# Gate products of a recurrent block as four 64x64 tiles, and a new order of transposes and conversions around them

## The chip, the cores and the metric

The kernel runs on one core of a Trainium2 chip. Its metric is the device time of one execution in microseconds; three executions of the kernel before give 296.25 us (median; 296.24 to 296.85). TensorE, VectorE, ScalarE, GpSimd and the DMA queue of SyncE each run their own list of instructions in order and meet at semaphores.

## The reference

One transformer layer on 256 tokens of width 1024, all in float32. Cut to what matters here:

```python
h = rms_norm(x, mix_norm_g)
xr, yg, q, k, v = split(h @ w_in)                      # 5 parts of 512 channels
xr = causal_depthwise_conv(xr, lru_conv_w, lru_conv_b)
r = sigmoid(einsum('bshi,hij->bshj', xh, w_a) + b_a)   # 8 heads, a 64x64 matrix each
i = sigmoid(einsum('bshi,hij->bshj', xh, w_i) + b_i)
a = exp(-8 * r * softplus(-lam));  u = sqrt(1 - a*a) * (i * xr)
y_lru = scan(a, u) * gelu(yg)                          # h[t] = a[t] h[t-1] + u[t]
y_attn = causal attention of 8 heads of 64 with distance slopes, q and k normed
x = x + concat(rms_norm(y_lru), rms_norm(y_attn)) @ w_out
x = x + (gelu(gate) * value) @ w_down                  # from rms_norm(x) @ w_up, convolved
```

## The kernel before, in words

Every weight matrix comes in units of 128 x 1024 numbers (0 to 93), two to a DMA of SyncE. A unit u is split into two parts of lower precision: `hi(u)` on ScalarE (L355) and `lo(u)` on VectorE (L652 and L656); VectorE makes both parts of units 17 to 22. A product of float32 accuracy is then three fast matmuls (`three`, L1001, L1002, L1005). TensorE waits for `lo_done` before it uses a unit. Units 0 to 7 are q and k, 8 to 11 the recurrent input, 12 to 15 the GELU branch y, 16 to 19 v, 20 to 27 w_out, 28 on the feed-forward part, whose loop takes the time behind 112 us.

The order of each engine is written out by hand. Around the change it is as follows.

TensorE computes y unit 0, then the gate products (`gates_product`, L1102): for each chunk c of 128 channels (two heads) one float32 matmul for the gate r and one for the gate i, with a 128x128 stationary operand that holds the two heads' 64x64 matrices on its diagonal and zeros elsewhere, and 256 tokens as columns. Both go to one PSUM bank, `X_ACC[c]`, r in columns 0 to 255, where the recurrent input of the chunk was until the convolution (`conv_rest`, L731) had read it. Then come pairs of heads' scores (`score_pair`, two heads on the two halves of the rows), y units, v units and the transposes of the probabilities (`transpose_p(h)`, L1099, three 128x128 blocks of a head). `score_pair(h)` waits until `shift` of the heads before has read the banks.

A head's probabilities pass these steps: `shift(h)` on VectorE (L746: add the distances, row minimum), `exps(h)` on ScalarE (L430), the division by the row sum (on GpSimd, L345, for heads 0 to 3; `row_scale(h)` on VectorE, L758 and L761, for the others), `transpose_p(h)` on TensorE, and `p_out(h)` on ScalarE (L436), the copy out of PSUM. The probabilities have five slots, so `shift(5)` waits for the transpose of head 0 (semaphore `pT`), `shift(6)` for that of head 1 and `shift(7)` for that of head 2. The transposed heads share two banks: `transpose_p(h)` waits for `p_out(h - 2)`.

The recurrence passes these: sigmoids on ScalarE (L471 and L473); `gate_i * xc` on VectorE (L801, `lru_in`); decay and tanh on ScalarE (L479, L480), their square (L485, `a2_done`); on VectorE the product that gives 1 - a^2 up to the sign (L807); the root on ScalarE (L494); on VectorE (L818, L820, L824) the scan's input, four scans and the product with GELU (`y_done`). `y_to_hi(c)` (L503) and `y_to_lo(c)` (L829) split chunk c of it for w_out and count `mix_ready`; `y_sq` (L515) and `chunk_sums` (L834, L835) give the sums of squares, which `y_sums` on TensorE adds up at w_out's second unit. For the attention half the same is done by L524, `chunk_sums` again (`a_chunks`) and `a_sums` (L1166) at the third unit. `v_out(m)` (L511) copies v out of PSUM; the second half of the attention products (`attend`, L1188) waits for `v_out(1)`.

Behind w_out, `f_add` (L879) adds the result to x, its norm follows, and `transpose_f` (L1222) turns it for the feed-forward part.

Of the kernel before, what the change touches and what calls it, by code (L numbers as in the profile page):

```python
# [30 lines left out]
P = 128  # L31
D_MODEL = 1024
SEQ = 256
# [66 lines left out]
def build_layer(nc, x, stream, params, gates, out):  # L100
    with ExitStack() as ctx:
# [157 lines left out]

        def f_at(m, kc):  # L260

            tile, at = (bank[kc // 4], kc % 4) if m == 0 else (bank[2 + kc % 4], kc // 4)
            return tile[:, P * at:P * (at + 1)]
# [85 lines left out]
        def _(act):  # L349
# [76 lines left out]
            def exps(h):  # L426
                act.wait_ge(shifted, h + 1)
                for m in range(TT):
                    part = slice(KEY_AT[m], KEY_AT[m] + KEYS[m])
                    act.activation(probs[h % P_SLOTS][:, part], probs[h % P_SLOTS][:, part], ACT.Exp, scale=-1.0,  # L430
                                   bias=neg_max[:, h, m:m + 1],
                                   accum_out=row_sum[:, h, m:m + 1]).then_inc(probs_done, 1)

            def p_out(h):
                act.wait_ge(pT, h + 1)
                act.activation(p_T[:, h, :], P_BANK[h % 2][:, 0:SCORES], ACT.Copy).then_inc(pT_read, 1)  # L436
# [32 lines left out]
            for c in range(LC):  # L469
                act.wait_ge(gates_done, c + 1)  # L470
                act.activation(gate_r[:, c, :], X_ACC[c][:, 0:SEQ], ACT.Sigmoid,  # L471
                               bias=par[:, B_A + c:B_A + c + 1])
                act.activation(gate_i[:, c, :], X_ACC[c][:, SEQ:2 * SEQ], ACT.Sigmoid,  # L473
                               bias=par[:, B_I + c:B_I + c + 1]).then_inc(gates_read, 1)
            exps(4)
            act.wait_ge(log_c_done, 1)
            act.wait_ge(gates_read, LC)
            for c in range(LC):
                act.activation(decay[:, c, :], gate_r[:, c, :], ACT.Exp, scale=log_c[:, c:c + 1])  # L479
                act.activation(tanh_a[:, c, :], gate_r[:, c, :], ACT.Tanh,  # L480
                               scale=log_c[:, c:c + 1]).then_inc(decay_done, 1)
                if c < 2:
                    p_out(c)
            act.wait_ge(decay_done, LC)
            act.activation(flat(gate_r), flat(decay), ACT.Square).then_inc(a2_done, 1)  # L485
            exps(5)
            p_out(2)
            p_out(3)
# [25 lines left out]
            act.wait_ge(y_done, 1)  # L514
            act.activation(y_sq, flat(ygate), ACT.Square).then_inc(y_sq_done, 1)  # L515
            v_out(1)
            y_to_hi(0)
            y_to_hi(1)
# [119 lines left out]
        def _(dve):  # L638
# [165 lines left out]
            los(17, 18)  # L804

# [3 lines left out]
            row_scale(5)  # L809
            shift(6)  # L810
            shift(7)
# [13 lines left out]
            los(21)  # L825
# [10 lines left out]

            dve.wait_ge(y_sq_done, 1)
            chunk_sums(y_pairs, y_sq_sum, y_sq, y_chunks)
            y_to_lo(0)
            y_to_lo(1)  # L840
# [157 lines left out]
        def _(pe):  # L998
# [104 lines left out]
            def gates_product(c):  # L1103

                pe.wait_ge(conv_done, c + 1)
                pe.matmul(X_ACC[c][:, 0:SEQ], w_gate[:, 0, c, :], xc[:, c, :], start=True, stop=True)  # L1106
                pe.matmul(X_ACC[c][:, SEQ:2 * SEQ], w_gate[:, 1, c, :], xc[:, c, :], start=True,  # L1107
                          stop=True).then_inc(gates_done, 1)
# [17 lines left out]
            y_unit(0)  # L1126
            pe.wait_ge(gates_landed, 16)
            for c in range(LC):
                gates_product(c)
            score_pair(4)  # L1130
            y_unit(1)
            transpose_p(0)
            transpose_p(1)
            y_unit(2)
            transpose_p(2)
            transpose_p(3)
            score_pair(6)
            y_unit(3)
            transpose_p(4)
            transpose_p(5)  # L1140
            rows_unit(U_V, U_V, V_ACC)
            transpose_p(6)
            transpose_p(7)
            rows_unit(U_V + 1, U_V, V_ACC)
            rows_unit(U_V + 2, U_V, V_ACC)
# [252 lines left out]
```

## Time and profile before

| | us |
|---|---|
| median of three executions | 296.25 |
| the profiled execution | 296.02 |
| its span, first to last instruction | 294.3 |
| TensorE busy | 288.4 |
| VectorE busy | 241.7 |
| ScalarE busy | 201.4 |
| GpSimd busy | 11.8 |

All positions in time below are microseconds from the start of the span. Busy time of TensorE counts overlapped ends, so two instructions that start 0.12 us apart may each last 0.28. What an instruction costs in a row of its kind is therefore the distance of the starts. The granted TensorE clock is 1.000 over the whole span, which is 2.4 GHz.

### The profile page before, as it was taken

The numbers are of one execution on the slowest core, as the hardware profiler recorded it, in microseconds if no ns is written. First come the engines' busy times: TensorE is split into PE (matmuls) and PEld (weight loads), VectorE is DVE, ScalarE is ACT, GpSimd is POOL, SyncE is SP. The second block draws the span as 40 slices with busy tenths as digits, with TensorE's granted clock in tenths as the row PEclk, the third lists the DMA queues.
The fourth block names the chain that finished last, engine by engine and source line by source line (L and its number), as shares of the span: only waits on it lengthen the run. The fifth ranks groups of instructions, "written<-read, shape, count | busy, mean of one in ns | idle before, by whom it ended". The sixth has DMA issues, their size and how long they took to land.

```text
span 294.3 us, 4943 instructions
## 1 busy us (share of the span) xinstructions
PE 288.4 (98%) x1630; PEld 249.9 (85%) x1630; DVE 241.7 (82%) x438; ACT 201.4 (68%) x371; POOL 11.8 (4%) x29
## 2 busy tenths in 40 slices
PE   7999999999999999999999999999999999999995
PEld 7788999898788799888888888888888888888884
DVE  2998497898999677999978888888788888888864
ACT  5975498989694488888666666676666666776540
POOL 4000000900000000000000000000000000000000
PEclk9999999999999999999999999999999999999999
DMA  7999942132264702564747544453746544200004
GB/s 241 431 417 424 416 160 72 72 143 76 77 237 183 288 1 66 222 247 180 287 143 249 182 154 165 166 229 143 285 143 237 190 158 157 112 0 0 0 0 145
DMA packets 8127, 52.22 MB, mean 177 GB/s; under 512 B 912, under 2 KB 1168, under 8 KB 2224
## 3 DMA queue, kind: packets, MB, share of 16 engines
q1 hardware_dynamic: 7920, 51.38, 46.6%
q0 software_dynamic: 192, 0.64, 0.6%
q8 instruction: 9, 0.15, 0.2%
q14 instruction: 6, 0.05, 0.1%
HBM read 50.98 MB, written 1.05 MB: 177 GB/s over the span
## 4 chain that ended last, share of the span: by engine, by line
PE 94%; DMA 2%; DVE 1%; ACT 1%; issue 0%; SPq 0%; ACTq 0%; DVEq 0%
PE bank L1285 26%; PE bank L1001 16%; PE bank L1002 15%; PE bank L1005 15%; PE bank L1289 14%; DMA raw<-in_stream_dram 2%; PE bank L1257 1%; PE bank L1072 1%; PE bank L1188 1%; PE bank L1265 1%; PE bank L1099 1%; PE bank L1222 1%; PE bank L1066 1%; PE bank L1106 1%; PE bank L1107 1%; ACT p_T L540 0%
## 5 line engine op out<-in xcount | busy, mean ns | idle before, releaser
L656 DVE TENSOR_TENSOR w_lo<-raw,w_hi 128x1024 fp32r<-128x1024 f32 x93 | 111.0, 1221 | 8.0 <-ACT w_hi L355 7.3
L355 ACT ACTIVATE w_hi<-raw 128x1024 fp32r<-128x1024 f32 x87 | 89.0, 1056 | 5.5 <-PE bank L1005 4.5
L1285 PE MATMUL bank<-h_both,w_hi 128*128 128x512 f32 x336 | 83.6, 391 | 0.0
L1285 PEld LDWEIGHTS bank<-h_both,w_hi 128*128 128x128 f32 x336 | 61.6, 188 | 11.8
L1289 PEld LDWEIGHTS bank<-h_both,w_lo 128*128 128x128 f32 x336 | 45.8, 190 | 3.3
L1289 PE MATMUL bank<-h_both,w_lo 128*128 128x256 f32 x336 | 46.9, 282 | 0.0
L581 ACT ACTIVATE tanh_a<-bank 128x256 f32<-128x256 f32 x44 | 16.8, 382 | 40.8 <-PE bank L1289 40.1
L1002 PE MATMUL bank<-w_lo,act_hi 128*128 128x512 f32 (+1 forms) x90 | 34.8, 387 | 0.0
L1001 PE MATMUL bank<-w_hi,act_hi 128*128 128x512 f32 (+1 forms) x90 | 34.8, 387 | 0.0
L1005 PE MATMUL bank<-w_hi,act_lo 128*128 128x512 f32 (+1 forms) x90 | 34.6, 384 | 0.0
L589 ACT ACTIVATE xc<-ygate,par 128x256 f32<-128x256 f32 x44 | 26.2, 596 | 3.2 <-DVE ygate L929 3.1
L929 DVE TENSOR_TENSOR ygate<-bank,tanh_a 128x256 f32<-128x256 f32 x44 | 18.5, 421 | 11.9 <-ACT tanh_a L581 11.9
L940 DVE SCALAR_TENSOR_TENSOR xc<-ygate,par,xc 128x254 f32<-128x254 f32 x44 | 21.3, 483 | 5.1 <-DVE xc L936 0.2
L936 DVE SCALAR_TENSOR_TENSOR xc<-ygate,par,xc 128x255 f32<-128x255 f32 x44 | 21.2, 481 | 3.4 <-ACT xc L589 3.2
L1005 PEld LDWEIGHTS bank<-w_hi,act_lo 128*128 128x128 f32 x90 | 16.9, 188 | 3.5
L1001 PE MATMUL bank<-w_hi,h_both 128*128 128x512 f32 x48 | 19.0, 395 | 0.7 <-DVE h_both L683 0.7
L1001 PEld LDWEIGHTS bank<-w_hi,act_hi 128*128 128x128 f32 x90 | 17.0, 189 | 2.9
L1002 PEld LDWEIGHTS bank<-w_lo,act_hi 128*128 128x128 f32 x90 | 17.0, 189 | 2.6
L1005 PE MATMUL bank<-w_hi,h_both 128*128 128x512 f32 x48 | 18.7, 390 | 0.0
L1002 PE MATMUL bank<-w_lo,h_both 128*128 128x512 f32 x48 | 18.7, 389 | 0.0
L1001 PE MATMUL bank<-h_both,w_hi 128*128 128x256 f32 x64 | 18.7, 292 | 0.0
L1005 PE MATMUL bank<-h_both,w_lo 128*128 128x256 f32 x64 | 18.1, 283 | 0.0
(163 smaller groups left out, 390.2 us busy)
## 6 DMA issues: line engine op xcount, KB each, us to landing
raw<-in_stream_dram SPq DMA_DIRECT2D x46, 1024.0 KB, 4.8
x_tok<-in_x_dram SPq DMA_DIRECT2D x2, 512.0 KB, 3.8
raw<-in_stream_dram SPq DMA_DIRECT2D x2, 512.0 KB, 6.9
out_dram<-x_tok SPq DMA_DIRECT2D x3, 256.0 KB, 2.4
p_T<-in_gates_dram POOLq DMA_DIRECT2D x1, 512.0 KB, 9.0
out_dram<-x_tok SPq DMA_DIRECT2D x2, 128.0 KB, 2.3
par<-in_params_dram POOLq DMA_DIRECT2D x1, 117.0 KB, 4.9
```

The source lines that it names most:

```text
L355: act.activation(w_hi[u % RING][:, :], raw_unit(u), ACT.Copy).then_inc(hi_done, 1)
L581: act.activation(cross[which][s % 2], up_bank(s, which)[:, SEQ:2 * SEQ], ACT.Copy).then_inc(cross_out, 1)
L589: act.activation((conv_g, conv_v)[which][s % 2], joined[which][s % 2], ACT.Identity, bias=par[:, bass.ds(col + FFN_B, 1)], scale=par[:, ba ...
L656: dve.tensor_tensor(w_lo[u % RING][:, :], raw_unit(u), w_hi[u % RING][:, :].bitcast(F32), ALU.subtract).then_inc(lo_done, 1)
L929: dve.tensor_tensor(joined[which][s % 2], up_bank(s, which)[:, 0:SEQ], cross[which][s % 2], ALU.add).then_inc((joined_g, joined_v)[which], 1)
L936: dve.scalar_tensor_tensor(acc[:, 1:SEQ], joined[which][s % 2][:, 0:SEQ - 1], par[:, bass.ds(col + (FFN_W + 2 * STEPS), 1)], acc[:, 1:SEQ] ...
L940: dve.scalar_tensor_tensor(acc[:, 2:SEQ], joined[which][s % 2][:, 0:SEQ - 2], par[:, bass.ds(col + FFN_W, 1)], acc[:, 2:SEQ], ALU.mult, AL ...
L1001: pe.matmul(acc, lhs_hi, rhs_hi, start=first, stop=False, skip_group_check=resumed)
L1002: pe.matmul(acc, lhs_hi, rhs_lo, start=False, stop=False, skip_group_check=resumed)
L1005: return pe.matmul(acc, lhs_lo, rhs_hi, start=False, stop=last, skip_group_check=resumed)
L1285: pe.matmul(acc[:, :], whi[:, kc, :], h_both[:, kc, :, :].rearrange("p b t -> p (b t)"), start=kc == 0, stop=False)
L1289: ins = pe.matmul(acc[:, 0:SEQ], wlo[:, kc, :], h_hi[:, kc, :], start=False, stop=kc == KC - 1)
```

## The change

The gate products of a chunk become four float32 matmuls of 64 rows by 64 columns, one for each gate and head, each on its own quarter of the array, with no zeros multiplied. So that the four use four different quarters, the product of gate i of the even head goes to partitions 64 to 127, and that of the odd head to partitions 0 to 63. ScalarE puts the halves back as it takes the sigmoid: gate i in two instructions of 64 partitions, each reading the other half. Gate r and gate i of a chunk now lie in two different banks, shared with the other chunk of the same parity, so the products of the first chunk wait for all four convolutions, and the chunks are taken in the order 0, 2, 1, 3.

On TensorE `score_pair(4)` moves ahead of the gates and `transpose_p(0)` to `transpose_p(7)` behind later units. On ScalarE `exps(5)`, `p_out(2)` and `p_out(3)` move ahead of the square of the decays, and `y_to_hi(0)` ahead of `v_out(1)`, `y_sq` behind `y_to_hi(1)`. On VectorE `row_scale(5)`, `shift(6)` and `shift(7)` move ahead of the wait for that square, and `y_to_lo(0)` and `y_to_lo(1)` ahead of the sums of squares.

```diff
+        def gate_acc(g, c):
+            at = SEQ * (1 - c // 2)
+            return X_ACC[2 * (c % 2) + g][:, at:at + SEQ]
...
-            for c in range(LC):
-                act.wait_ge(gates_done, c + 1)
-                act.activation(gate_r[:, c, :], X_ACC[c][:, 0:SEQ], ACT.Sigmoid,
-                               bias=par[:, B_A + c:B_A + c + 1])
-                act.activation(gate_i[:, c, :], X_ACC[c][:, SEQ:2 * SEQ], ACT.Sigmoid,
-                               bias=par[:, B_I + c:B_I + c + 1]).then_inc(gates_read, 1)
+            for n, c in enumerate(GATE_ORDER):
+                act.wait_ge(gates_done, 2 * (n // 2) + 2)
+                act.activation(gate_r[:, c, :], gate_acc(0, c), ACT.Sigmoid, bias=par[:, B_A + c:B_A + c + 1])
+                for rows, swapped in ((slice(0, HALF), slice(HALF, P)), (slice(HALF, P), slice(0, HALF))):
+                    ins = act.activation(gate_i[rows, c, :], gate_acc(1, c)[swapped, :], ACT.Sigmoid,
+                                         bias=par[rows, B_I + c:B_I + c + 1])
+                ins.then_inc(gates_read, 1)
             exps(4)
+            p_out(0)
+            p_out(1)
+            exps(5)
             act.wait_ge(log_c_done, 1)
             act.wait_ge(gates_read, LC)
             for c in range(LC):
                 act.activation(decay[:, c, :], gate_r[:, c, :], ACT.Exp, scale=log_c[:, c:c + 1])
                 act.activation(tanh_a[:, c, :], gate_r[:, c, :], ACT.Tanh,
                                scale=log_c[:, c:c + 1]).then_inc(decay_done, 1)
-                if c < 2:
-                    p_out(c)
+                if c == 1:
+                    p_out(2)
+                    p_out(3)
             act.wait_ge(decay_done, LC)
             act.activation(flat(gate_r), flat(decay), ACT.Square).then_inc(a2_done, 1)
-            exps(5)
-            p_out(2)
-            p_out(3)
...
             act.wait_ge(y_done, 1)
+            y_to_hi(0)
+            v_out(1)
+            y_to_hi(1)
             act.activation(y_sq, flat(ygate), ACT.Square).then_inc(y_sq_done, 1)
-            v_out(1)
-            y_to_hi(0)
-            y_to_hi(1)
...
             row_scale(4)
-            los(17, 18)
-
+            los(17)
+            row_scale(5)
+            los(18)
+            shift(6)
+            shift(7)
             dve.wait_ge(a2_done, 1)
             dve.scalar_tensor_tensor(flat(tanh_a), flat(gate_r), 1.0, flat(tanh_a), ALU.add,
                                      ALU.mult).then_inc(one_m_a2, 1)
-            row_scale(5)
-            shift(6)
-            shift(7)
...
-            los(21)
...
+            y_to_lo(0)
+            los(21)
+            y_to_lo(1)
             dve.wait_ge(y_sq_done, 1)
             chunk_sums(y_pairs, y_sq_sum, y_sq, y_chunks)
-            y_to_lo(0)
-            y_to_lo(1)
...
-                pe.wait_ge(conv_done, c + 1)
-                pe.matmul(X_ACC[c][:, 0:SEQ], w_gate[:, 0, c, :], xc[:, c, :], start=True, stop=True)
-                pe.matmul(X_ACC[c][:, SEQ:2 * SEQ], w_gate[:, 1, c, :], xc[:, c, :], start=True,
-                          stop=True).then_inc(gates_done, 1)
+                pe.wait_ge(conv_done, LC)
+                even, odd = slice(0, HALF), slice(HALF, P)
+                for g, rows, cols in ((0, even, even), (1, odd, even), (1, even, odd), (0, odd, odd)):
+                    ins = pe.matmul(gate_acc(g, c)[cols, :], w_gate[rows, g, c, rows], xc[rows, c, :], start=True, stop=True)
+                ins.then_inc(gates_done, 1)
...
             y_unit(0)
+            score_pair(4)
             pe.wait_ge(gates_landed, 16)
-            for c in range(LC):
+            for c in GATE_ORDER:
                 gates_product(c)
-            score_pair(4)
             y_unit(1)
+            y_unit(2)
             transpose_p(0)
             transpose_p(1)
-            y_unit(2)
+            score_pair(6)
+            y_unit(3)
             transpose_p(2)
             transpose_p(3)
-            score_pair(6)
-            y_unit(3)
+            rows_unit(U_V, U_V, V_ACC)
             transpose_p(4)
             transpose_p(5)
-            rows_unit(U_V, U_V, V_ACC)
+            rows_unit(U_V + 1, U_V, V_ACC)
+            rows_unit(U_V + 2, U_V, V_ACC)
             transpose_p(6)
             transpose_p(7)
-            rows_unit(U_V + 1, U_V, V_ACC)
-            rows_unit(U_V + 2, U_V, V_ACC)
```

## Rows read from the trace of the kernel before

**Rows 1.** The page's busy times, and the engines' shares of its last chain.
```profile
PE 288.4 (98%) x1630; PEld 249.9 (85%) x1630; DVE 241.7 (82%) x438; ACT 201.4 (68%) x371; POOL 11.8 (4%) x29
...
PE 94%; DMA 2%; DVE 1%; ACT 1%; issue 0%; SPq 0%; ACTq 0%; DVEq 0%
```

**Rows 2.** TensorE's timeline, 49 to 58 us: start, duration, engine, line, operation, count.
```profile
49.98 0.60 PE L1106 MATMUL bank<-xc,p_T 128*128 128x256 f32 x2
...
53.53 0.93 PE L1072 MATMUL bank<-k_T,q_T 64*128 64x128 f32 x8
54.39 0.38 PE L1001 MATMUL bank<-h_both,w_hi 128*128 128x256 f32 x1
...
57.37 0.82 PE L1099 MATMUL bank<-ident,qk_tok 128*128 128x128 f32 x6
57.94 0.36 PE L1001 MATMUL bank<-h_both,w_hi 128*128 128x256 f32 x1
```

**Rows 3.** TensorE's timeline: a score pair's first records, and all attention products.
```profile
42.23 0.38 PE L1072 MATMUL bank<-k_T,q_T 64*128 64x128 f32 x2
...
77.84 2.82 PE L1188 MATMUL bank<-p_T,v_tok 128*64 128x256 f32 x32
```

**Rows 4.** TensorE's timeline: a_sums, the first piece for f_add(0), transpose_f(0).
```profile
86.81 0.50 PE L1166 MATMUL bank<-ones,k_T 128*128 128x1 f32 x4
...
97.29 0.39 PE L1005 MATMUL bank<-w_hi,mix_lo 128*128 128x512 f32 x1
...
101.40 1.09 PE L1222 MATMUL bank<-ident,decay 128*128 128x128 f32 x8 [0.32 <-ACT decay L550]
```

**Rows 5.** ScalarE's timeline, 53 to 79 us.
```profile
53.10 0.47 ACT L471 ACTIVATE gate_r<-bank,par 128x256 f32<-128x256 f32 x1
...
55.60 0.52 ACT L473 ACTIVATE gate_i<-bank,par 128x256 f32<-128x256 f32 x1
...
57.43 0.40 ACT L430 ACTIVATE qk_tok<-qk_tok,small 128x128 f32<-128x128 f32 x1
...
58.33 0.49 ACT L479 ACTIVATE decay<-gate_r,small 128x256 f32<-128x256 f32 x1
...
62.39 1.06 ACT L485 ACTIVATE gate_r<-decay 128x1024 f32<-128x1024 f32 x1
...
64.24 0.84 ACT L436 ACTIVATE p_T<-bank 128x384 f32<-128x384 f32 x2
...
78.75 1.70 ACT L503 ACTIVATE mix_hi<-ygate,par 128x256 fp32r<-128x256 f32 x4
```

**Rows 6.** VectorE's timeline, 49 to 98 us.
```profile
49.41 1.51 DVE L731 SCALAR_TENSOR_TENSOR xc<-bank,par,xc 128x255 f32<-128x255 f32 x3
...
56.96 1.22 DVE L801 TENSOR_TENSOR gate_i<-gate_i,xc 128x1024 f32<-128x1024 f32 x1
58.10 0.28 DVE L746 CUSTOM_DVE_ANT_0 qk_tok<-bank,neg_dist 128x128 f32<-128x128 f32 x1
...
58.65 0.16 DVE L758 RECIPROCAL small<-small 128x2 f32<-128x2 f32 x1
...
59.31 0.69 DVE L652 CAST w_hi<-raw 128x1024 fp32r<-128x1024 f32 x1
...
63.49 1.23 DVE L807 SCALAR_TENSOR_TENSOR tanh_a<-gate_r,tanh_a 128x1024 f32<-128x1024 f32 x1 [0.36 <-ACT gate_r L485]
...
68.53 0.68 DVE L652 CAST w_hi<-raw 128x1024 fp32r<-128x1024 f32 x1
...
72.25 1.22 DVE L818 TENSOR_TENSOR gate_r<-tanh_a,gate_i 128x1024 f32<-128x1024 f32 x1
...
76.05 1.23 DVE L824 TENSOR_TENSOR ygate<-tanh_a,ygate 128x1024 f32<-128x1024 f32 x1
...
85.42 0.42 DVE L835 TENSOR_TENSOR k_T<-k_T 128x256 f32<-128x256 f32 x1
...
97.79 1.41 DVE L879 SCALAR_TENSOR_TENSOR x_tok<-bank,small,x_tok 128x512 f32<-128x512 f32 x2 [0.61 <-PE bank L1005]
```

More of the change, by code:

```diff
@@ L31 @@
 P = 128
+HALF = P // 2
 D_MODEL = 1024
@@ L258, in x_at @@
             return bank[2 + kc][:, 0:SEQ] if kc < 4 else bank[6 + (kc - 4) // 2][:, SEQ * (kc % 2):SEQ * (kc % 2 + 1)]
+        GATE_ORDER = (0, 2, 1, 3)
+        def gate_acc(g, c):
+            at = SEQ * (1 - c // 2)
+            return X_ACC[2 * (c % 2) + g][:, at:at + SEQ]
         def f_at(m, kc):
```

## The prediction

> **What bounds the kernel now.** The shares come first: TensorE is busy 288.4 of 294.3 us and holds 94% of the chain that ended last [rows 1]. So an instruction taken off TensorE is worth its time, but only until TensorE has to wait for something. The second view is therefore TensorE's timeline over the changed stretch, to see what each piece costs [rows 2]; then the timelines of ScalarE [rows 5] and VectorE [rows 6], to see how much later each may be before TensorE waits; and last TensorE's own late instructions, which consume what those two make [rows 4]. The reader is to see in rows 5 and 6 that both engines run nearly without a gap from 49 to 86 us. VectorE waits 0.36 us at 63.49 and 0.61 us at 97.79, and only some tenths between [rows 6]. It is a second chain, as long as TensorE's, and it ends in a_sums: VectorE has the attention squares' sum at 85.42 + 0.42 = 85.84, and TensorE asks for it at 86.81 [rows 4, 6]. That slack is 0.93 us. The next one is at f_add(0), 0.61 us.
>
> **The gate products.** Now 16 records (two for each float32 product) take 49.98 to 53.53, 3.55 us, of which about 0.1 is the step into the tiled scores [rows 2]; so 3.45 us, or 0.216 a record. In the change 16 products of 64x64 make 32 records of as many columns. No row shows four tiles at once. Two at once are shown: the first two records of a score pair, on the two row halves, stand together in 0.38 us, the length of one [rows 3]; the attention's 32 records of 64 output columns take 2.82 us [rows 3], where 16 of 256 columns and 16 of 128 one behind another would take 16 x 0.216 + 16 x 0.108 = 5.2. Bounds: all serial 6.9 us, two at once 3.45, four at once 1.73. I take four: both kinds of pairing are full in the rows, and the four tiles of the change differ in row half or column half. The order then has one more step between tilings, since scores now precede gates: a tiled stretch costs TensorE about 0.4 us beside its records (0.86 + 0.1 in + 0.1 in the unit behind it, against 0.64 of columns) [rows 2], a second tiling inside the stretch about half of it, 0.2. So TensorE saves 3.45 - 1.73 - 0.2 = 1.5 us of its own.
>
> The Trainium skill ("TensorEngine Tiling (Array Packing)", Restrictions and Gotchas, Gotcha 1) says that different row tiles cannot access the same PSUM bank at the same time. Here the input gate's halves are exchanged, so the even row half writes partitions 0-63 of bank g = 0 while the odd row half writes 64-127 of it. Taken literally only two tiles would run together, and that is the second case below. No row of this kernel has two row tiles in one bank: the score pairs use two.
>
> **TensorE's new timetable.** y0 ends at 49.98. Score pair 4 with its entry is 0.95, to 50.93. The gates wait for all four convolutions: VectorE ends the last at 49.41 + 1.51 = 50.92 [rows 6], before it was asked for one by one; nothing lost, since only the 0.04 us of a semaphore is late. Gates to 52.7, y1 from 52.8. A y unit is 2.98 us [rows 2], about 2.88 when it follows another directly (the 0.1 of the first record is not paid), so transpose_p(0) stands at 58.65, where before it stood at 57.37. Its output is there at 59.15 (0.82 for six transposes, less the 0.33 of the second head).
> Here the new wait is. shift(5) on VectorE reuses the slot of head 0 and needs that transpose; before it ran at 58.10, now at 59.19, and is out 0.64 later, 59.83 [rows 6]. score_pair(6), now directly behind transpose_p(1), needs it: TensorE waits about 0.5 us, and has it done at 60.73 (0.86). y3 to 63.7, transposes 2 and 3 from there, the first out at 64.2.
>
> **ScalarE.** The input gates take two instructions of 64 partitions for one of 128. One of 128 costs (55.60 - 53.10) / 7 = 0.357 us, seven starts later [rows 5]. The price of 64 partitions is between half of that and all of it; I take all, so +4 x 0.357 = 1.43 us, sigmoids ending near 57.6. The end is nearly the same by either, for two steps on ScalarE waits anyway. Table load (1.3, from 55.60 + 0.52 to 57.43) and exps(4) (0.90, 57.43 to 58.33) go on to 59.8, p_out(0), p_out(1) take 0.74 (0.84 - 0.47 = 0.37 each), exps(5) 0.90, the first four of the eight decays 1.6: ScalarE is at p_out(2) at 63.0 and waits 1.2 us for transpose 2, until 64.2. Then two p_outs 0.74, four decays 1.6 (each (62.39 - 58.33 - 0.74 - 0.14) / 8 = 0.40), 0.14 for the last to drain, square 1.06: a2_done at 67.8, before 62.39 + 1.06 = 63.45 [rows 5]. It comes 4.3 us later: 1.43 more sigmoids, 0.90 exps(5), 0.74 p_out(2, 3), 1.2 waiting.
>
> **VectorE.** Before a2_done the change puts row_scale(5), shift(6) and shift(7) ahead of the wait; they are hidden in it. lru_in waits for the gates 0.6, shift(5) for transpose 0 0.46, and with row_scale(4, 5) 0.66 each, two units of 1.86 and the shifts VectorE is at the wait at 66.0 and sits idle 1.8 us, until 67.8. From there: product 1.14 (as 56.96 to 58.10), row_scale(6, 7) 1.3, units 19 and 20 3.72 (68.53 to 72.25), so the scan's input begins at 73.96 instead of 72.25 [rows 6]: 1.7 us late. Root and GELU are ready before it is needed: behind a2_done ScalarE has exps(6, 7) 1.8, two p_outs 0.74 and a table load 1.3, so the root is done near 72.7; another load and the two GELUs end near 75.1, and they are wanted at 77.7. y_done is 76.05 + 1.23 + 1.7 = 78.97, before 77.28.
> Behind it, ScalarE gives y_to_hi(0) first (0.5; its four take 1.70 with 0.40 between starts [rows 5]) and VectorE y_to_lo(0) at 79.55. That takes mix_ready(1) to y_done + 1.1, where now it is y_done + 3.3, and pays for TensorE's first W_out unit. But VectorE's whole work from y_done to the attention's squares is the same 8.65 us (76.05 + 1.14 = 77.19 to 85.84 [rows 6]), and now starts 2.36 late, 1.7 of it from y_done and 0.66 because y_to_lo(0) has no unit 21 to hide ScalarE's step behind. a_chunks come at 88.20.
>
> **What TensorE meets.** The second half of the attention products needs v_out(1), which ScalarE now issues behind y_to_hi(0): 78.97 + 0.04 + 0.4 + 0.58 = 80.0; TensorE is there at about 78.6 and waits 1.4 us, which is where its 1.5 us go. W_out begins at 81.1 (now 80.75), and a_sums at 88.24 (now 86.81): +1.43. VectorE is free for f_add(0) at 97.79 - 0.61 - 0.07 + 2.36 = 99.5; TensorE's piece for it is there at 97.29 + 0.39 + 1.43 = 99.1, so VectorE ends last, f_add(0) is at 99.5 and 1.7 late [rows 4, 6]. From there each step hangs on the one before: TensorE already waits for the norm's scaling at 101.40 (0.32 in the row) [rows 4], and the loop behind it is TensorE's. Nothing gives it back. Sum: +1.7 us, 296.0 + 1.7 = 297.7 against the profiled execution's own 296.02; the median of the runs is 0.23 above that, so 297.95. Gates that cost nothing at all would still leave +1.25, and a three-quarter overlap (2.6 us) +2.6: that is the likeliest case's own range, 297.2 to 298.9.
>
> **The rivals.**
> Two tiles at a time. The gates take 3.45, TensorE has y1 1.72 later, and through transposes 0 and 2 everything behind it too: +3.4, 299.7. For it speaks that no row shows more than two at once, and the two row halves meeting in one bank; against it that tiles of different halves were never seen to hinder each other. All serial: +6.9, 303.1; rows 3 speak against it.
> The shorter tail pays. TensorE enters W_out now at 80.75, hardly 0.1 after the first y chunk could be ready, so it is bound by y there, and the change takes 2.2 us out of that step. If that were the one place that ties TensorE to y, and ScalarE's late square were caught up by VectorE, the 1.5 us would stay: 294.8. It decides at a_chunks: TensorE without waits would ask for them at 85.3, with the 0.5 before score pair 6 lost at 85.8; my timetable has 88.2. For it VectorE must not be idle before a2_done, so a2_done must come near 65.5, which needs transpose 2 before y3 or no wait of ScalarE for it. The rows speak against it.
> No change: half of my lateness is absorbed because the units on VectorE are a bit shorter or the wait at p_out(2) is; that leaves at most 0.5 us.
>
> **How the numbers follow.** Four tiles and the late y chain 0.63; two tiles 0.17; serial 0.03; gain stays 0.08; within the noise 0.09. Predicted is the first, 297.95. The range 296.7 to 299.9 takes in the first two, with the bounds of the gates' price between four and two tiles. About 0.2%, 0.6 us, is what a measurement can tell from no change: slower 0.82, same 0.09, faster 0.09.
>
> **What would show it.** Gate records: four within 0.03 us and 1.7 us in all (two tiles: 3.4). TensorE's stops: 0.5 before score pair 6, 1.4 in the middle of the attention products, 1.3 before a_sums. ScalarE idle 1.2 before p_out(2). VectorE idle 1.8 before the product on tanh_a, and no wait left before f_add(0). Squares of the decay ending at 67.8, ygate's product at 79. If the square ends before 66, or VectorE's wait is under 0.5, the forecast is wrong.

## The result: 2.6 us slower, and the profile after

The changed kernel takes 298.79 us (median of 22 executions), the kernel before beside it 296.23 (22 executions): a ratio of 1.0089, 95% interval 1.0074 to 1.0103, or +2.6 us where +1.7 was predicted. The profiled execution took 299.3 us with a span of 297.5; the granted clock is 1.000 throughout. In some executions of most kernels the mean granted clock is 0.99 instead of 1.00 and the time up to some 3 us longer; medians and ratios take them in, and do not always agree to the last tenth of a per cent for that reason.

One correction comes ahead of every reading. What TensorE does in front of the changed stretch is the same code in all kernels, yet it ends between 50.0 and 51.6 us in the profiled executions. (The four kernels whose names begin with c also move a few conversions of ScalarE and VectorE to places in front of it.) So positions are compared from the start of score pair 4. In the kernel before, where the gates stand in its place, that is 50.07: 49.98 of [rows 2] and the 0.09 of the step into a tiled stretch. "From the score pair" below means this distance. In the kernel before a_sums lies at 86.81 - 50.07 = 36.74 [rows 4] and f_add(0) at 97.79 - 50.07 = 47.72 [rows 6].

The page first: its busy times, and the engines' shares of the last chain, as in [rows 1].
```profile
PE 287.0 (96%) x1646; PEld 247.6 (83%) x1646; DVE 241.6 (81%) x438; ACT 204.2 (69%) x375; POOL 11.0 (4%) x29
...
PE 64%; DVE 3%; ACT 1%; issue 0%; ACTq 0%
```
TensorE has 1.4 us less work, and the kernel is slower. ScalarE has 2.8 us more. TensorE's share of the chain went from 94% to 64%; only part of the rest is given to other engines, so this line says that the chain no longer stays on TensorE, not by how much. The timelines say that.

TensorE's timeline of the changed kernel (start, duration, engine, line, operation, count, and in brackets the idle time in front and what ended it):
```profile
50.95 0.93 PE L1082 MATMUL bank<-k_T,q_T 64*128 64x128 f32 x8
51.95 1.96 PE L1118 MATMUL bank<-xc,p_T 64*64 64x256 f32 x32
53.83 0.39 PE L1011 MATMUL bank<-h_both,w_hi 128*128 128x256 f32 x1
...
59.96 0.85 PE L1109 MATMUL bank<-ident,qk_tok 128*128 128x128 f32 x6
61.68 0.93 PE L1082 MATMUL bank<-k_T,q_T 64*128 64x128 f32 x8 [0.88 <-DVE small L756]
...
81.92 1.09 PE L1199 MATMUL bank<-p_T,v_tok 128*64 128x128 f32 x16 [1.41 <-ACT v_tok L521]
...
90.12 0.61 PE L1177 MATMUL bank<-ones,k_T 128*128 128x1 f32 x4 [0.90 <-DVE k_T L844]
```
The 32 gate records lie in 53.83 - 51.95 = 1.88 us, the step out included, where the 16 of before took 3.55 [rows 2]. The first four stand within 20 ns of each other, and from the second group on four begin every 0.216 us, within 50 ns of each other: all four tiles run at once. But TensorE now stops for others 0.88 + 1.41 + 0.90 = 3.2 us between score pair 4 and a_sums, and a_sums is 39.17 from the score pair: +2.43. (Each stop costs 0.1 to 0.2 us more than its idle time, since the ends of records drawn here overlap the next start; this, and 0.27 us ahead of the transposes of head 0 that is treated below, make up for the 1.4 us saved.)

ScalarE's timeline of the changed kernel, to be laid beside [rows 5]:
```profile
53.98 0.47 ACT L479 ACTIVATE gate_r<-bank,par 128x256 f32<-128x256 f32 x1
54.46 0.95 ACT L481 ACTIVATE gate_i<-bank,par 64x256 f32<-64x256 f32 x2
55.44 0.47 ACT L479 ACTIVATE gate_r<-bank,par 128x256 f32<-128x256 f32 x1
...
59.83 1.28 ACT L438 ACT_TABLE_LOAD   x1
...
66.05 0.88 ACT L444 ACTIVATE p_T<-bank 128x384 f32<-128x384 f32 x2 [0.71 <-PE bank L1109]
...
68.54 1.06 ACT L498 ACTIVATE gate_r<-decay 128x1024 f32<-128x1024 f32 x1
```
A chunk's three sigmoids take 55.44 - 53.98 = 1.46 us, 0.487 each. The eight of before stood 0.357 apart. All twelve, up to the table load behind them, take 59.83 - 53.98 = 5.85 us. The eight of before took 56.14 - 53.10 = 3.04, by this row of the kernel before:
```profile
56.14 1.28 ACT L430 ACT_TABLE_LOAD   x1
```
Four more at 0.357 would have made that 4.47.

VectorE's timeline of the changed kernel, to be laid beside [rows 6]:
```profile
59.85 1.23 DVE L811 TENSOR_TENSOR gate_i<-gate_i,xc 128x1024 f32<-128x1024 f32 x1 [1.92 <-ACT gate_i L481]
...
69.63 1.22 DVE L820 SCALAR_TENSOR_TENSOR tanh_a<-gate_r,tanh_a 128x1024 f32<-128x1024 f32 x1 [1.24 <-ACT gate_r L498]
...
75.81 1.22 DVE L828 TENSOR_TENSOR gate_r<-tanh_a,gate_i 128x1024 f32<-128x1024 f32 x1
...
79.61 1.23 DVE L834 TENSOR_TENSOR ygate<-tanh_a,ygate 128x1024 f32<-128x1024 f32 x1
81.41 0.48 DVE L838 SCALAR_TENSOR_TENSOR mix_lo<-ygate,par,mix_hi 128x256 fp32r<-128x256 f32 x1 [0.58 <-ACT mix_hi L513]
...
89.65 0.42 DVE L844 TENSOR_TENSOR k_T<-k_T 128x256 f32<-128x256 f32 x1
...
101.32 1.40 DVE L889 SCALAR_TENSOR_TENSOR x_tok<-bank,small,x_tok 128x512 f32<-128x512 f32 x2
```
It waits 1.92 for the sigmoids and 1.24 for the square. From the score pair the scan's input lies at 75.81 - 50.95 = 24.86 (before 22.18) and f_add(0) at 50.37: +2.65, with nothing idle in front, where before VectorE waited 0.61 for TensorE. That +2.65 is the 2.6 us of the comparison.

### The profile page after: what moved, and what is told of

Read it like the earlier page. It is cut to its first block, busy times and chain, and to the rows that moved or that the text cites. A ratio compares the mean times of both kernels' runs of the same rounds, so it can differ in the third digit from the quotient of the medians.

```text
span 297.5 us, 4979 instructions
## 1 busy us (share of the span) xinstructions
PE 287.0 (96%) x1646; PEld 247.6 (83%) x1646; DVE 241.6 (81%) x438; ACT 204.2 (69%) x375; POOL 11.0 (4%) x29
## 4 chain that ended last, share of the span: by engine, by line
PE 64%; DVE 3%; ACT 1%; issue 0%; ACTq 0%
PE bank L1296 26%; PE bank L1300 13%; PE bank L1011 7%; PE bank L1012 7%; PE bank L1015 7%; PE bank L1268 1%; DVE w_lo L666 1%; DVE x_tok L875 1%; PE bank L1276 1%; PE bank L1233 1%; ACT p_T L550 0%; DVE x_tok L889 0%; ACT decay L560 0%; DVE x_tok L1004 0%; DVE h_both L915 0%
## 5 line engine op out<-in xcount | busy, mean ns | idle before, releaser
L1300 PE MATMUL bank<-h_both,w_lo 128*128 128x256 f32 x336 | 46.9, 282 | 0.0
L1011 PE MATMUL bank<-h_both,w_hi 128*128 128x256 f32 x64 | 18.6, 291 | 0.0
L1012 PE MATMUL bank<-h_both,w_hi 128*128 128x256 f32 x64 | 18.1, 283 | 0.0
```

Source lines behind the costliest of these rows:

```text
L1011: pe.matmul(acc, lhs_hi, rhs_hi, start=first, stop=False, skip_group_check=resumed)
L1012: pe.matmul(acc, lhs_hi, rhs_lo, start=False, stop=False, skip_group_check=resumed)
L1300: ins = pe.matmul(acc[:, 0:SEQ], wlo[:, kc, :], h_hi[:, kc, :], start=False, stop=kc == KC - 1)
```

## The experiments

Three kernels ask what the sigmoids cost, two what tiles and orders do apart, one for the new order of the tail, and four whether TensorE's saving can reach the end at all. Their results together (us; the first two columns are positions in the profiled execution, from the score pair, with the difference to before):

| kernel | a_sums | f_add(0) | median | ratio to before, 95% |
|---|---|---|---|---|
| before | 36.74 | 47.72 | | |
| the change | 39.17 (+2.43) | 50.37 (+2.65) | 298.79 | 1.0074 to 1.0103 |
| s1_whole | 38.51 (+1.77) | 49.70 (+1.98) | 298.34 | 1.0016 to 1.0092 |
| s2_halves | 38.65 (+1.91) | 49.84 (+2.12) | 299.2 | one execution |
| s3_grouped | 38.53 (+1.79) | 49.72 (+2.00) | 297.96 | 1.0019 to 1.0077 |
| s4_gates_only | 39.74 (+3.00) | 50.71 (+2.99) | 299.51 | 1.0056 to 1.0130 |
| s5_orders_only | 39.95 (+3.21) | 51.13 (+3.41) | 300.42 | 1.0054 to 1.0193 |
| s6_tail_old | 39.37 (+2.63) | 50.34 (+2.62) | 300.19 | 1.0056 to 1.0181 |
| c1_filled | 35.99 (-0.75) | 46.97 (-0.75) | 295.88 | 0.9954 to 1.0035 |
| c2_filled_full | 37.17 (+0.43) | 48.14 (+0.42) | 296.91 | 0.9978 to 1.0054 |
| c3_early_out | 35.23 (-1.51) | 46.20 (-1.52) | 295.19 | 0.9925 to 0.9973 |
| c4_early_out_full | 36.59 (-0.15) | 47.56 (-0.16) | 296.31 | 0.9963 to 1.0006 |

The kernel before took 296.44 beside the first four, 296.36 beside s5 to c2, 296.45 beside the last two. Where an interval is wide (s5, s6, c1, c2), the positions in the trace carry the reading, which is then one execution's.

### What the sigmoids cost

s1_whole takes the sigmoid of gate i in one instruction of 128 partitions; the halves of gate i stay exchanged, so it leaves that part of the computation out.
```diff
-                for rows, swapped in ((slice(0, HALF), slice(HALF, P)), (slice(HALF, P), slice(0, HALF))):
-                    ins = act.activation(gate_i[rows, c, :], gate_acc(1, c)[swapped, :], ACT.Sigmoid,
-                                         bias=par[rows, B_I + c:B_I + c + 1])
+                ins = act.activation(gate_i[:, c, :], gate_acc(1, c), ACT.Sigmoid, bias=par[:, B_I + c:B_I + c + 1])
```


> The changed kernel with gate i taken in one instruction of 128 partitions, halves not put back (so the two heads' input gates stand exchanged); everything else as in the change. Theory: the added time is the delay of the ScalarE-VectorE chain, and its part above my 1.7 us comes from the sigmoids, which took 0.487 us each in all twelve instead of 0.357. Then the eight sigmoids here stand 0.357 apart (last one 2.5 us behind the first), VectorE's wait for the gates falls from 1.92 to near 0, and the kernel is about 1.0 us faster than the change: +1.7 us over the kernel before, 297.9. Rival (the new order of the transposes alone makes the delay, the sigmoids are hidden by ScalarE's later wait for transpose 2): same as the change, +2.6.

s2_halves keeps two instructions of 64 partitions, but each reads its own half (the halves stay exchanged here too).
```diff
-                    ins = act.activation(gate_i[rows, c, :], gate_acc(1, c)[swapped, :], ACT.Sigmoid,
+                    ins = act.activation(gate_i[rows, c, :], gate_acc(1, c)[rows, :], ACT.Sigmoid,
```


> The changed kernel with gate i in two instructions of 64 partitions, but each reading its own half (gates exchanged between heads). Tells what broke the overlap of the sigmoids. If it is the crossing of partitions: 64-partition instructions at 0.357, and the stage ends 1.5 us sooner than in the change. If it is that neighbouring instructions cover different partitions, or 64 of them: 0.487 for each, stage as in the change (first sigmoid to table load 5.85 us), time +2.6 us. I expect the second.

s3_grouped computes what the change computes, in another order: four times r, then the lower halves of the four i, then the upper.
```diff
-            for n, c in enumerate(GATE_ORDER):
-                act.wait_ge(gates_done, 2 * (n // 2) + 2)
+            act.wait_ge(gates_done, LC)
+            for c in range(LC):
                 act.activation(gate_r[:, c, :], gate_acc(0, c), ACT.Sigmoid, bias=par[:, B_A + c:B_A + c + 1])
-                for rows, swapped in ((slice(0, HALF), slice(HALF, P)), (slice(HALF, P), slice(0, HALF))):
+            for rows, swapped in ((slice(0, HALF), slice(HALF, P)), (slice(HALF, P), slice(0, HALF))):
+                for c in range(LC):
```


> The changed kernel, same results, with the sigmoids in three groups: gate r of all chunks (128 partitions), then gate i of all chunks into partitions 0-63, then into 64-127, so that neighbours cover the same partitions. If only a change of partitions costs the overlap: 0.357 within a group and 0.487 at the two borders, the stage takes 4.4 + 0.26 = about 4.6 us instead of 5.85, and the kernel is 0.9 to 1.0 us faster than the change: +1.7 over before. If 64-partition instructions never overlap: about 5.4 us, +2.3.

ScalarE's timeline of s1_whole:
```profile
53.57 0.48 ACT L479 ACTIVATE gate_r<-bank,par 128x256 f32<-128x256 f32 x1
...
56.61 1.28 ACT L438 ACT_TABLE_LOAD   x1
...
59.82 0.87 ACT L444 ACTIVATE p_T<-bank 128x384 f32<-128x384 f32 x2 [0.92 <-PE bank L1107]
...
64.98 0.87 ACT L444 ACTIVATE p_T<-bank 128x384 f32<-128x384 f32 x2 [1.78 <-PE bank L1107]
```
of s2_halves:
```profile
54.40 0.47 ACT L479 ACTIVATE gate_r<-bank,par 128x256 f32<-128x256 f32 x1
54.77 0.94 ACT L481 ACTIVATE gate_i<-bank,par 64x256 f32<-64x256 f32 x2
55.74 0.47 ACT L479 ACTIVATE gate_r<-bank,par 128x256 f32<-128x256 f32 x1
...
59.74 1.28 ACT L438 ACT_TABLE_LOAD   x1
```
and of s3_grouped:
```profile
53.19 1.57 ACT L479 ACTIVATE gate_r<-bank,par 128x256 f32<-128x256 f32 x4
54.77 3.11 ACT L482 ACTIVATE gate_i<-bank,par 64x256 f32<-64x256 f32 x8
57.90 1.28 ACT L438 ACT_TABLE_LOAD   x1
...
64.61 0.87 ACT L444 ACTIVATE p_T<-bank 128x384 f32<-128x384 f32 x2 [1.20 <-PE bank L1111]
```
Half the partitions save nothing: 0.47 us long like the whole. What differs is whether the next instruction may begin before this one has ended. In s2_halves it does so from r to the lower half (54.77 - 54.40 = 0.37), both starting at partition 0; from the lower half to the upper and from there to the next r it does not ((55.74 - 54.77) / 2 = 0.485). In the change either the input or the output starts at another partition than that of the instruction in front, every time: 0.487 throughout. Grouped, nine of the twelve follow one with the same starts, and the stage takes 57.90 - 53.19 = 4.71 us instead of 5.85. The expectation for s2_halves, 0.487 for each of the twelve, was not met: its stage takes 59.74 - 54.40 = 5.34 us. The Trainium skill ("ScalarE: Activation LUTs", What ACT_TABLE_LOAD costs) says that "Back-to-back ACTIVATEs overlap by ≈ 93 ns". The traces have 0.10 to 0.16 us of it where the starts stay, and none where they change.

The end results are the instructive part. Both s1_whole and s3_grouped were expected about 1.0 us faster than the change; at f_add(0) they are 0.67 and 0.65. From s1_whole to s3_grouped ScalarE has four instructions more, and a_sums does not move: 38.51 and 38.53. Two of its waits absorb them instead: the one for the transposes of head 0, ahead of p_out(0), goes from 0.92 us to nothing, and the one for those of head 2, ahead of p_out(2), from 1.78 to 1.20. From s3_grouped to the change the stage is 1.14 us longer; the same wait gives 0.49 (1.20 to 0.71), and f_add(0) moves by the other 0.65.

### Tiles and orders apart

s4_gates_only is the change with the orders of before (score pair 4 still ahead of the gates). s5_orders_only is the change with the full products and the sigmoids of before.
```diff
+            p_out(0)
+            p_out(1)
+            exps(5)
...
             y_unit(1)
+            y_unit(2)
             transpose_p(0)
             transpose_p(1)
-            y_unit(2)
+            score_pair(6)
+            y_unit(3)
             transpose_p(2)
```
These lines show which way s5_orders_only goes from before; s4_gates_only leaves all moves of the change's diff away but that of score pair 4.

> The kernel before with the four-tile gates and the exchanging sigmoids alone (score pair 4 ahead of them, as in the change); all other orders as before. Theory (what ends last is the chain gates_read - VectorE - y_done, which has no slack): TensorE gains 1.5 us in the gates and loses it at transpose_p(0), where it waits about 3.2 us for the sigmoids; VectorE waits 2.0 us for the gates, a2_done comes 2.8 us later, and the kernel is 2.6 us slower than before, as slow as the change. Rival (the new order is the cause and the gates a gain): 1.5 us faster than before, 294.7.

> The changed kernel with its new orders on all engines, but the gate products and sigmoids of the kernel before (eight full matmuls, eight sigmoids of 128 partitions). Theory: transposes 0 and 2 stand behind y units and are late by the whole of the gates (3.45 us), so shift(5) on VectorE, score pair 6, p_out(2), a2_done and y_done follow: 3.2 us slower than before, 299.5, with the waits of VectorE for transpose 0 at 2.6 and of ScalarE for transpose 2 at 1.8 us. Rival (only the exchanging sigmoids cost): no slower than before.

TensorE's timeline of s4_gates_only:
```profile
59.55 1.51 PE L1108 MATMUL bank<-ident,qk_tok 128*128 128x128 f32 x6 [3.00 <-ACT gate_i L481]
...
61.51 0.41 PE L1010 MATMUL bank<-h_both,w_hi 128*128 128x256 f32 x1
61.72 0.41 PE L1011 MATMUL bank<-h_both,w_hi 128*128 128x256 f32 x1
...
62.72 0.28 PE L1010 MATMUL bank<-h_both,w_hi 128*128 128x256 f32 x1
...
64.51 0.82 PE L1108 MATMUL bank<-ident,qk_tok 128*128 128x128 f32 x6
```
and its stretches (busy time of PE, its weight loads, DVE, ACT, POOL, then the granted clock, DMA share, GB/s):
```profile
56.60:60.00 3.40, 0.45 (x2) 0.47 (x3) 1.44 (x7) 3.31 (x7) 2.10 (x3) 0.88 0.00 0
60.00:62.00 2.00, 2.00 (x12) 2.00 (x11) 1.44 (x7) 1.99 (x6) 0.00 (x0) 0.50 0.00 0
62.00:64.00 2.00, 2.00 (x16) 2.00 (x16) 1.97 (x4) 2.00 (x7) 0.00 (x0) 0.85 0.00 0
```
and VectorE's timeline of it:
```profile
59.44 1.23 DVE L810 TENSOR_TENSOR gate_i<-gate_i,xc 128x1024 f32<-128x1024 f32 x1 [1.93 <-ACT gate_i L481]
...
79.36 1.23 DVE L833 TENSOR_TENSOR ygate<-tanh_a,ygate 128x1024 f32<-128x1024 f32 x1
```
TensorE's transposes of head 2 in the kernel before:
```profile
60.90 0.82 PE L1099 MATMUL bank<-ident,qk_tok 128*128 128x128 f32 x6
```
VectorE's timeline of s5_orders_only:
```profile
62.37 0.29 DVE L755 CUSTOM_DVE_ANT_0 qk_tok<-bank,neg_dist 128x128 f32<-128x128 f32 x1 [2.69 <-PE bank L1108]
71.02 1.23 DVE L819 SCALAR_TENSOR_TENSOR tanh_a<-gate_r,tanh_a 128x1024 f32<-128x1024 f32 x1 [1.85 <-ACT gate_r L497]
```
The tiles alone cost 3.0 us, on two chains at once. On TensorE, the transposes of heads 0 and 1 go to banks 6 and 7, two of the four where the gates lie, so `transpose_p(0)` waits for all sigmoids (`gates_read`). With one y unit between the gates and it, TensorE stops for 3.00 us. That also is why the transposes have to be later if the gates are short. The granted clock falls to 0.50, the level of 1.2 GHz, at 59.2 us, late in the stop, and is back at 62.6: records that stand 0.12 us apart elsewhere stand 0.21 apart. From the transposes of head 0 to those of head 2 it takes 64.51 - 59.55 = 4.96 us, where before took 60.90 - 57.37 = 3.53: 1.4 us more. Not much of it seems to reach the end: the one execution of ten that kept a mean clock of 0.999 took 299.08 us, against a median of 299.5 for the nine others. The second chain is that of the recurrence, and it is as late by itself: the sigmoids take 2.8 us more than in before, VectorE waits 1.93 for them, and y's product begins at 79.36 - 50.53 = 28.83 from the score pair, where before has 76.05 - 50.07 = 25.98, +2.85. The change's own stops, of up to 1.41 us, left the clock at 1.000.

The orders alone cost 3.4 us. With the long gates, head 0 is transposed at 61.73, and VectorE's `shift(5)`, placed ahead of everything that leads to the scan, waits 2.69 us for it; then 1.85 for the square, which ScalarE has late for the same reason. Together, tiles and orders cost 2.65, less than either alone: the short gates bring head 0's transposes forward for the new orders, and the new orders put a second y unit in front of them, under which most of the wait for the sigmoids is hidden. Neither pays.

### The order of the tail

s6_tail_old puts `y_sq` and the sums of squares back ahead of the splits of y, as in before.
```diff
-            y_to_hi(0)
-            v_out(1)
-            y_to_hi(1)
             act.activation(y_sq, flat(ygate), ACT.Square).then_inc(y_sq_done, 1)
+            v_out(1)
+            y_to_hi(0)
+            y_to_hi(1)
```


> The changed kernel with the order behind y_done as before (square first on ScalarE, unit 21 and the sums first on VectorE). My step: putting y_to_lo(0) ahead costs VectorE 0.6 us of waiting and only moves where TensorE waits. Expected then: VectorE's idle 0.58 before y_to_lo(0) gone, TensorE's wait before a_sums gone and 0.6 at w_out's first unit instead, f_add(0) 0.2 to 0.3 us sooner than in the change; time +2.4 us against before. Rival (the new tail helps, since mix_ready comes 2.2 us sooner): slower than the change by about 1 us, +3.6.

TensorE's timeline of s6_tail_old:
```profile
81.97 1.09 PE L1199 MATMUL bank<-p_T,v_tok 128*64 128x128 f32 x16 [1.96 <-ACT v_tok L521]
83.81 0.47 PE L1011 MATMUL bank<-w_hi,mix_hi 128*128 128x512 f32 x1 [0.74 <-DVE mix_lo L838]
...
89.85 0.50 PE L1177 MATMUL bank<-ones,k_T 128*128 128x1 f32 x4
```
and VectorE's f_add(0) in it:
```profile
100.82 1.41 DVE L889 SCALAR_TENSOR_TENSOR x_tok<-bank,small,x_tok 128x512 f32<-128x512 f32 x2 [0.58 <-PE bank L1015]
```
The tail's new order moves TensorE's stops: 1.96 + 0.74 become 1.41 + 0.90. At a_sums it is worth 0.20 us, at f_add(0) nothing (50.34 against 50.37). That the two agree there is two effects of like size: with the old order VectorE no longer waits 0.58 us ahead of `y_to_lo(0)` (81.41 in the change), is ready for f_add(0) 0.6 us sooner, and then waits 0.58 us for TensorE; in the change VectorE is the one that is last. The expectation, 0.2 to 0.3 us sooner, was not met for that reason.

This holds for an execution at full clock. The comparison says something else: the profiled execution is the fastest of four, 298.82 us at a clock of 1.000; the three others took 299.97, 300.40 and 301.32 at mean clocks of 0.993, 0.994 and 0.989, and their median with it is 1.4 us above that of the change, of whose 22 executions two had such a clock. One stretch at half clock, as in the trace of s4_gates_only, gives a mean of 0.994. Whether the longer stop of 1.96 us brings it on, or four executions are too few, no trace shows. So it is open whether the new order of the tail is worth something in the mean.

### Can the saving reach the end?

c1_filled has the tiles and the grouped sigmoids, the tail of before, and orders made so that neither ScalarE nor VectorE has to wait on the way to the square. On ScalarE the decays stand between the copies of the transposes and `exps(5)`; on VectorE each `shift` has units in front of it; TensorE transposes head 2 ahead of score pair 6. Beside the lines shown, `his(16)` goes ahead of `exps(2)`, `p_out(3)` behind the square, `p_out(4)` behind the root, `p_out(5)` behind the Gelus, and `transpose_p(4)` ahead of the first v unit. c2_filled_full is the same with the gates and sigmoids of before.
```diff
             exps(4)
+            decays(0)
             p_out(0)
             p_out(1)
+            decays(1)
+            decays(2)
+            p_out(2)
+            decays(3)
             exps(5)
...
+            shift(4)
+            los(17)
...
-            shift(5)
-            row_scale(4)
-            los(17)
-            row_scale(5)
             los(18)
+            row_scale(4)
+            shift(5)
+            los(19)
             shift(6)
             shift(7)
+            row_scale(5)
+            los(20)
...
             transpose_p(0)
             transpose_p(1)
-            score_pair(6)
             y_unit(3)
             transpose_p(2)
+            score_pair(6)
             transpose_p(3)
```


> A version meant to beat both: four-tile gates, sigmoids grouped by partitions, and orders chosen so that the two engines of the second chain don't wait: VectorE makes units 17 to 20 while it would wait (17 before the gates' constants, 18 before row_scale(4), 19 and 20 before the late product), ScalarE makes unit 16 before exps(2), and decays stand between the p_outs; score pair 6 behind y unit 3 and transposes 0 to 2; tail as before. By the theory VectorE's waits between the gates and the scan sum to under 1 us instead of 4.4, TensorE keeps its 1.5 us and never waits over 0.3: 294.8 (-1.4 us). Rival (VectorE's chain is as long as TensorE's whatever its order): no gain, 296.2.

> The same orders as c1_filled with the gates and sigmoids of the kernel before. If the gain of c1_filled is TensorE's shorter gates, this one has none: TensorE is the bound, -0.1 us, 296.1. If it came from the orders, this one has it as well.

TensorE's timeline of c1_filled:
```profile
50.26 0.93 PE L1086 MATMUL bank<-k_T,q_T 64*128 64x128 f32 x8
...
59.01 0.82 PE L1113 MATMUL bank<-ident,qk_tok 128*128 128x128 f32 x6
...
74.22 0.52 PE L1113 MATMUL bank<-ident,qk_tok 128*128 128x128 f32 x3 [0.63 <-ACT p_T L444]
```
and of c2_filled_full:
```profile
51.32 0.93 PE L1075 MATMUL bank<-k_T,q_T 64*128 64x128 f32 x8
...
61.49 0.82 PE L1102 MATMUL bank<-ident,qk_tok 128*128 128x128 f32 x6
```
These rows give TensorE's saving with the same two y units in between and no stop: from score pair 4 to the transposes of head 0 it is 59.01 - 50.26 = 8.75 us with tiles and 10.17 without. The tiles save 1.42 us on TensorE, steps between tilings included; 1.5 was predicted. Of it 0.75 reached f_add(0) in the trace, where -1.4 was expected; the comparison alone cannot tell c1_filled from before. Most of the rest stands in the last of c1_filled's rows: the transposes of head 7 waited 0.63 us for `p_out(5)`, which stood behind the Gelus and their table load. In c2_filled_full the same wait is 0.36 of its +0.42.

c3_early_out and c4_early_out_full move that copy ahead.
```diff
             p_out(4)
+            p_out(5)
...
-            p_out(5)
```


> The kernel c1_filled with one call moved: ScalarE copies out the probabilities' transposes of head 5 before the Gelus instead of behind them. In c1_filled TensorE waited 0.63 us at the transposes of head 7, whose bank this copy gives back, because the copy stood behind a table load of 1.28 and Gelus of 0.97; that was its only wait between score pair 4 and a_sums. Theory (with ScalarE and VectorE kept off the path, TensorE's own saving on the gates, 1.57 less 0.2 for the second change of tiling, reaches the end): a_sums and f_add(0) another 0.6 nearer to score pair 4, at 35.4 and 46.35 after its start, so 1.3 to 1.4 us under before in the trace and about 1.2 to 1.4 in the comparison (295.0 beside 296.3). VectorE's product y still ends behind the scans, as its Gelus come 0.4 later than in c1_filled and were 2 us early. Rival (two tiles at a time, or a cost of the tiles that the gates' own records don't show): no faster than before, 296.3 or more.

> The same orders as c3_early_out with the full 128x128 gate products and the four whole sigmoids of before. Theory: this separates tiles from orders. Of c2_filled_full's +0.42 in the trace the wait of 0.36 at the transposes of head 7 goes: a_sums and f_add(0) within 0.2 of their places in before, a time within 0.3 us of before, and 1.2 to 1.4 us above c3_early_out. If the orders alone made c3_early_out fast, this kernel would be as fast as it.

In c3_early_out TensorE does not stop once between score pair 4 (50.03) and a_sums, and VectorE waits for TensorE again at f_add(0). TensorE's a_sums and VectorE's f_add(0) in it:
```profile
85.26 0.50 PE L1181 MATMUL bank<-ones,k_T 128*128 128x1 f32 x4
...
96.23 1.41 DVE L893 SCALAR_TENSOR_TENSOR x_tok<-bank,small,x_tok 128x512 f32<-128x512 f32 x2 [0.58 <-PE bank L1019]
```
It is 1.52 us ahead of before in the trace and 295.19 against 296.45 us in the comparison, 1.3 us by the medians; the ratio is 0.9949 (0.9925 to 0.9973). The slowest of its twelve executions, 296.12, is faster than 20 of the 23 of before. With the full gates the same orders give 296.31, the time of before. The tiles, with their grouped sigmoids, make the 1.1 us (1.36 in the trace) between them; of the orders alone the trace shows 0.16. How much of this would be left with the sigmoids in the change's alternating order was not run.

## Why the prediction came out as it did

The direction and the mechanism held; one term was too small, and one wait was not seen. Positions from the score pair, predicted (less 50.07) and measured:

| step | predicted | the change | s3_grouped |
|---|---|---|---|
| transposes of head 0 | 8.58 | 9.01 | 8.74 |
| score pair 6 | 9.80 | 10.73 | 10.08 |
| square begins | 16.67 | 17.59 | 16.93 |
| scan's input begins | 23.89 | 24.86 | 24.21 |
| attention sum ready (a_chunks) | 38.13 | 39.12 | 38.48 |
| a_sums | 38.17 | 39.17 | 38.53 |
| f_add(0) | 49.43 | 50.37 | 49.72 |

**The gates on TensorE.** Four tiles at once, right; 1.42 us saved for 1.5. The rival with two tiles at a time is out. The Trainium skill ("TensorEngine Tiling (Array Packing)", Restrictions and Gotchas, Gotcha 1) forbids two row tiles in one bank at the same time; here the two wrote disjoint halves of the partitions, and the records show them together, with no delay.

**The sigmoids, the term that was mis-sized.** "I take all, so +4 x 0.357 = 1.43 us" should have been 5.85 - 3.04 = 2.81. The step that failed is taking the distance of the starts of eight instructions with one placement as the price of others with changing placement. The bound above was wrong with it: "between half of that and all of it" did not hold the value. And "the end is nearly the same by either" was right for the 1.43 us (s1_whole against s3_grouped: nothing), wrong for what came on top: of the 1.14 us between s3_grouped and the change 0.65 reached f_add(0).

**Where it was passed on.** VectorE's wait for the gates was 1.92 for a predicted 0.6, and took the place of that for transpose 0. The stop ahead of score pair 6 was 0.88 for 0.5, because `shift(5)` stood behind this wait. ScalarE's wait at p_out(2) was 0.71 for 1.2, VectorE's for the square 1.24 for 1.8: both shrank since all before them was later. In s3_grouped, where the stage takes 4.71 us, they are 0.77, 0.52, 1.20 and 1.74, the predicted sizes.

**A wait that the prediction did not see.** `transpose_p(0)` waits for the sigmoids, which cost the change 9.01 - 8.74 = 0.27 us, and in s4_gates_only 3.00. It stood in the code, before and after, on a bank that both use; before, the sigmoids were done when TensorE came there.

**What is left.** s3_grouped still has f_add(0) 0.29 later than predicted. The transposes of head 0 are 0.16 later; y unit 1 already begins 53.05 - 50.17 = 2.88 from the score pair for a predicted 2.73, so this lies in the steps between tilings. The square is 0.26 later, 0.10 of it behind them. What made that 0.10 is open.

**The tail.** The 1.41 us in the attention products, nothing idle ahead of f_add(0), y_done to a_chunks as before plus 0.6: as predicted. The wait ahead of a_sums was 0.90 for 1.3, TensorE having come later itself. The rival in which the shorter tail pays is out: it needed a_chunks by 85.8 - 50.07 = 35.7 from the score pair, and they came at 39.12. Its premise, that the 1.4 us stays if VectorE isn't late, is what c3_early_out shows in other orders.

## What to carry to other kernels

When TensorE is the bound and another engine has only 0.6 to 0.9 us of slack behind it, a shorter TensorE stage pays only if what it feeds gets earlier too; here the outputs of the gates became more expensive to read, and kernels with the same tiles were 2.6 us slower or 1.3 us faster than before, by the order of the work around them. Before moving work ahead of an engine's wait, follow that engine's chain to the next step that others need, and put the chain's own instructions first. Price sigmoids like these, which change their start partition from one to the next, at their full length, not at the distance at which their like follow each other.

## What the runs showed of the hardware

- ScalarE's sigmoids of 256 columns from PSUM follow each other at 0.357 us while inputs and outputs start at the same partition as in the one in front, and at 0.485 to 0.487 when one of them changes. 64 partitions cost what 128 do (0.47 us each).
- Four float32 matmuls of 64x64 on four quarters of the array run together: 32 records of 256 columns in 1.96 us, two row tiles in one bank included, on different partitions.
- In the trace of s4_gates_only TensorE's granted clock fell to 0.50 within a stop of 3.00 us and was back 3.4 us later; over stops of 0.52 to 1.96 us it stayed at 1.00 in the other profiled executions.
